# The new tokens' attention values: page values as the moving operand at four row positions

## The reference, cut to what matters

```python
def gather(pool):
    g = pool[page_table]                       # (8 samples, 2 pages, 128 rows, 8 heads, 64)
    return g.reshape((g.shape[0], g.shape[1] * g.shape[2]) + g.shape[3:])
# fox_attention, for one new token per sample
s = einsum('bqhd,bkhd->bhqk', q, k) * scale + fq - fk
p = softmax(s)
out = einsum('bhqk,bkhd->bqhd', p, v)          # (8 samples, 1, 8 heads, 64)
```

## Time and profile before

| | us |
|---|---|
| median of 3 runs (3226.53 to 3233.24) | 3230.78 |
| the profiled execution | 3236.48 |
| its span, first to last instruction | 3234.7 |
| TensorE matmul busy | 3023.7 (93%) |
| VectorE, ScalarE, GpSimd busy | 1567.6, 955.6, 1332.6 |
| mean granted TensorE clock | 0.969 |

### The profile page before, as it was taken

The page is one execution under the profiler, slowest core; times in us unless marked ns, Lnnn a source line. Parts: engine busy times, 40 slices in busy tenths (PEclk is TensorE's granted clock), DMA queues, the critical chain, the costliest instruction groups (busy, mean ns, idle before and its releaser), DMA issues.

```text
span 3234.7 us, 73556 instructions
## 1 busy us (share of the span) xinstructions
PE 3023.7 (93%) x32300; PEld 2845.5 (88%) x32300; DVE 1567.6 (48%) x2107; ACT 955.6 (30%) x1640; POOL 1332.6 (41%) x1016
## 2 busy tenths in 40 slices
PE   7999988989999999989999889999878999999997
PEld 6989856889999999978999877777777999999996
DVE  5032254237666641244322156688624866663125
ACT  4132264233111121123311246666623211111112
POOL 3322310235777743341433323333232677774320
PEclk9999998999999999999999889999989999999998
DMA  3344453322223233112422313222142122324311
GB/s 101 119 135 111 144 169 110 97 79 79 79 79 112 79 131 143 52 45 103 170 92 92 100 46 98 65 61 72 47 169 91 60 79 80 114 81 134 139 42 61
DMA packets 342471, 312.25 MB, mean 97 GB/s; under 512 B 35335, under 2 KB 303059, under 8 KB 341020
## 3 DMA queue, kind: packets, MB, share of 16 engines
q1 hardware_dynamic: 325706, 275.99, 28.3%
q10 hardware_dynamic: 16466, 31.83, 2.6%
HBM read 212.79 MB, written 94.62 MB: 95 GB/s over the span
## 4 chain that ended last, share of the span: by engine, by line
PE 43%; DVE 4%; issue 3%; ACT 1%; SPq 1%; DMA 1%; POOL 1%; ACTq 0%; DVEq 0%; POOLq 0%
PE PS L521 17%; PE PS L688 12%; PE PS L2799 2%; PE PS L2811 1%; PE PS L2805 1%; PE PS L2793 1%; DVE act_lo L2516 1%; PE PS L2919 1%; PE PS L2789 1%; PE PS L702 1%; PE PS L2785 1%; PE PS L2844 0%; SPq L496 0%; PE PS L2950 0%; PE PS L2980 0%
## 5 line engine op out<-in xcount | busy, mean ns | idle before, releaser
L521 PE MATMUL PS<-act_hi,w_hi 128*128 128x344 f32 x1992 | 641.0, 322 | 38.3 <-DVE act_lo L2150 21.2
L521 PE MATMUL PS<-act_lo,w_hi 128*128 128x344 f32 x1992 | 637.8, 320 | 0.0
L521 PE MATMUL PS<-act_hi,w_lo 128*128 128x344 f32 x1992 | 637.3, 320 | 0.0
L502 POOL CAST w_hi<-w_raw 128x1024 fp32r<-128x1024 f32 (+1 forms) x119 | 129.1, 1085 | 1078.4 <-PE PS L521 561.2
L521 PEld LDWEIGHTS PS<-act_hi,w_hi 128*128 128x128 f32 x1992 | 376.4, 189 | 43.4 <-issue 28.3
L521 PEld LDWEIGHTS PS<-act_hi,w_lo 128*128 128x128 f32 x1992 | 376.4, 189 | 0.0
L521 PEld LDWEIGHTS PS<-act_lo,w_hi 128*128 128x128 f32 x1992 | 376.4, 189 | 0.0
L688 PE MATMUL PS<-T,wq_S 128*128 128x258 f32 x2880 | 365.7, 283 | 0.0
L688 PE MATMUL PS<-act_hi,wq_A 128*128 128x258 f32 x1920 | 364.5, 282 | 0.0
L688 PEld LDWEIGHTS PS<-T,wq_S 128*128 128x128 f32 x2880 | 354.4, 189 | 0.0
L688 PEld LDWEIGHTS PS<-act_hi,wq_A 128*128 128x128 f32 x1920 | 305.4, 190 | 0.0
(11 more groups left out here) (603 smaller groups left out, 5852.0 us busy)
## 6 DMA issues: line engine op xcount, KB each, us to landing
hidd<-hid_out SPq DMA_DIRECT2D x44, 516.0 KB, 3.3
w_raw<-in_ffn_w_gate_dram SPq DMA_DIRECT2D x44, 512.0 KB, 4.8
w_raw<-in_ffn_w_up_dram SPq DMA_DIRECT2D x44, 512.0 KB, 6.0
w_raw<-in_ffn_w_down_dram SPq DMA_DIRECT2D x32, 512.0 KB, 4.1
hid_in<-hidd SPq DMA_DIRECT2D x28, 516.0 KB, 7.2
proj<-stage ACTq DMA_DIRECT2D x24, 516.0 KB, 2.7
xT<-xkeep SPq DMA_DIRECT2D x3, 4128.0 KB, 16.6
rw<-z_st SPq DMA_DIRECT2D x24, 516.0 KB, 2.8
```

Of the source, the lines that this page charges most:

```text
L502: nc.gpsimd.tensor_copy(w_hi[:, u, 0:kts, :], w_raw[:, u, 0:kts, :]).then_inc(w_hi_done, 1)
L521: mm = nc.tensor.matmul(PS[:, 3 * u + c, 0:CH], w[:, u, kt, :], x[:, kt, CH * c:CH * c + CH], start=(kt == 0 and part == 0), stop=(kt == k ...
```

## The change

In steps 28 and 31 the roles of the operands are swapped. The probabilities of one page (128 rows by 8 heads) are the stationary operand, and the page of values is the moving one, 512 columns. Four samples' results lie at the row positions 0, 32, 64 and 96 of one PSUM bank, eight rows (heads) each. Every head is multiplied with the values of all heads, so only a block diagonal of the result is wanted: VectorE multiplies with a head mask (`d_own`) into `d_mix`, and one step later (29 and 32) TensorE sums the rows of each sample and turns the result by a product with a constant (`d_seq`), 128 x 128 times 4 columns, four times. ScalarE then copies 128 x 16 into `d_of`. The marks `DV0`, `DV1` go from ScalarE to VectorE, and new marks `DG0`, `DG1` on TensorE and ScalarE take part in the ring. POOL and SP wait for `DG1` where they waited for `DV1`.

```diff
-            return names + {... 28: ["DV0"], 31: ["DV1"]}.get(j, [])
+            return names + {... 28: ["DV0"], 29: ["DG0"], 31: ["DV1"], 32: ["DG1"]}.get(j, [])
...
         def fox_end_sync(sp):
-            sp.wait_ge(FA.sem, FA["DV1"] + START)
+            sp.wait_ge(FA.sem, FA["DG1"] + START)
...
                 if j in (28, 31):
...
-                    for x in range(4):
-                        mm(PS[:, bank, 2 * (NS * x + 4 * h):2 * (NS * x + 4 * h + 4)], d_tm[:, 1024 + P * x:1024 + P * x + P],
-                           d_w2[:, x, 4 * h:4 * h + 4, :].rearrange("p b e -> p (b e)"), start=True, stop=False, skip_group_check=True)
-                        for i in range(8 * h, 8 * h + 8):
-                            b, p = i // NPAGES, i % NPAGES
-                            ins = mm(PS[:, bank, 2 * (NS * x + b):2 * (NS * x + b) + 2], d_v[i % 8][:, P * x:P * x + P],
-                                     d_pt[:, p, FH * b + 2 * x:FH * b + 2 * x + 2], start=False, stop=(i == 8 * h + 7), skip_group_check=True)
+                    mm(PS[:, bank, :], d_w2[:, h, :, :].rearrange("p b m -> p (b m)"), d_tm[:, 1024:1536], start=True, stop=False, skip_group_check=True)
+                    for p in range(NPAGES):
+                        for q in range(4):
+                            ins = mm(PS[32 * q:32 * q + FH, bank, :], d_pt[:, p, FH * (4 * h + q):FH * (4 * h + q) + FH], d_v[NPAGES * q + p][:, :],
+                                     start=False, stop=(p == NPAGES - 1), skip_group_check=True)
+                    ins.then_inc(FT.sem, 1)
+                if j in (29, 32):
+                    h = 0 if j == 29 else 1
+                    pe.wait_ge(FV.sem, FV[f"DV{h}"] + START)
+                    for x in range(4):
+                        ins = mm(PS[:, bank, 4 * x:4 * x + 4], d_mix[:, P * x:P * x + P], d_seq[:, :], start=True, stop=True)
                     ins.then_inc(FT.sem, 1)
...
-                if j in (28, 31):
-                    h = 0 if j == 28 else 1
-                    act.wait_ge(FT.sem, FT[f"DV{h}"] + START)
-                    out = PS[:, ring_bank(f"DV{h}"), 0:2 * NS * 4].rearrange("p (j b e) -> p j b e", j=4, e=2)
-                    for e in range(2):
-                        nc.scalar.copy(d_of[64 * e:64 * e + 64, :, 4 * h:4 * h + 4], out[64 * e:64 * e + 64, :, 4 * h:4 * h + 4, e]).then_inc(FA.sem, 1)
+                if j in (29, 32):
+                    h = 0 if j == 29 else 1
+                    act.wait_ge(FT.sem, FT[f"DG{h}"] + START)
+                    nc.scalar.copy(d_of[:, :, 4 * h:4 * h + 4], PS[:, ring_bank(f"DG{h}"), 0:16].rearrange("p (j b) -> p j b", j=4)).then_inc(FA.sem, 1)
...
                 if j == 27:
                     dve.wait_ge(d_wself_in, 16 + START)
-                    for x in range(4):
-                        c(tt(d_w2[:, x, :, :], ...), f"dw{x}")
+                    c(nc.vector.memset(d_w2[:, :, :, :], 0.0), "dwz")
+                    for h in range(2):
+                        c(tt(d_w2[:, h, :, 0:FH], ...), f"dw{h}")
+                    c(nc.vector.tensor_reduce(d_own[:, :], ident[:, :].rearrange("p (b t) -> p t b", b=4)[:, 0:FH, :], AX.X, ALU.add), "down")
+                    c(nc.vector.tensor_reduce(d_seq[:, :], ident[:, :].rearrange("p (b t) -> p b t", b=4)[:, :, 0:FH], AX.X, ALU.add), "dseq")
+                if j in (28, 31):
+                    h = 0 if j == 28 else 1
+                    dve.wait_ge(FT.sem, FT[f"DV{h}"] + START)
+                    if h:
+                        dve.wait_ge(FT.sem, FT["DG0"] + START)
+                    c(tt(d_mix[:, :].rearrange("p (h d) -> p h d", h=FH), PS[:, ring_bank(f"DV{h}"), :].rearrange("p (h d) -> p h d", h=FH),
+                         d_own[:, :].rearrange("p (h o) -> p h o", o=1).broadcast_to([P, FH, DH]), ALU.mult), f"DV{h}")
...
-            pool.wait_ge(FA.sem, FA["DV1"] + START)
+            pool.wait_ge(FA.sem, FA["DG1"] + START)
             split_pairs(pool, "out0", 4, KT)
```

More of the change, by code:

```diff
@@ L1266, in decoder_step @@
         d_pt = put("d_pt", [P, NPAGES, BF])
-        d_w2 = put("d_w2", [NS, 4, NS, 2])
-        assert places["d_w2"][2] <= 2 * ROW + 4 * TP
+        d_w2 = put("d_w2", [NS, 2, 4, 32])
+        d_own, d_seq = put("d_own", [P, FH]), put("d_seq", [P, 4])
+        assert places["d_seq"][2] <= 2 * ROW + 4 * TP
+        assert places["d_pr"][2] - places["d_sc"][1] >= 4 * FH * DH
+        d_mix = at("h", "d_mix", [P, FH * DH], places["d_sc"][1])
         d_page = [nc.alloc_sbuf_tensor_at(f"d_page{i}", [P, FH * DH], F32, offset=slots["w_hi" if i < 4 else "w_lo"] + 2048 * (i % 4)) for i in range(8)]
@@ L1702, in fox_tensor_names @@
                 names += [f"{n}{p + 1}.{h}" for n, h in KV_PARTS if n == "vk"[b - 1]]
-            return names + {3: ["DX0", "DX1", "DX2"], 22: ["DB"], 23: ["DS"], 26: ["DP"], 28: ["DV0"], 31: ["DV1"]}.get(j, [])
+            return names + {3: ["DX0", "DX1", "DX2"], 22: ["DB"], 23: ["DS"], 26: ["DP"], 28: ["DV0"], 29: ["DG0"], 31: ["DV1"], 32: ["DG1"]}.get(j, [])
         def fox_scalar_names(j):
@@ L1713, in fox_scalar_names @@
                 names += [f"{n}{p + 1}.{h}" for n, h in KV_PARTS if n == "vk"[b - 1]]
-            return names + {3: ["DX0", "DX1", "DX2"], 24: ["dexp"], 26: ["DP"], 28: ["dof0", "DV0"], 31: ["dof1", "DV1"]}.get(j, [])
+            return names + {3: ["DX0", "DX1", "DX2"], 24: ["dexp"], 26: ["DP"], 29: ["DG0"], 32: ["DG1"]}.get(j, [])
         FIRST_PAGE = 6
@@ L1722, in fox_vector_names @@
             names += [f"o{(j - 1) // 4}"] if j and j % 4 == 0 else []
-            names += {5: ["dqk", "dself"], 22: ["DB"], 23: ["DS", "dself8", "dmax", "dneg"], 25: ["dinv", "dpr"], 27: ["dw0", "dw1", "dw2", "dw3"]}.get(j, [])
+            names += {5: ["dqk", "dself"], 22: ["DB"], 23: ["DS", "dself8", "dmax", "dneg"], 25: ["dinv", "dpr"], 27: ["dwz", "dw0", "dw1", "down", "dseq"], 28: ["DV0"], 31: ["DV1"]}.get(j, [])
             names += [f"{n}{j - FIRST_PAGE}" for n in ("kq", "sc")] if 0 <= j - FIRST_PAGE < NP else []
@@ L1899, in sample @@
             def sample(j):
-                name = {22: "DB", 23: "DS", 26: "DP", 28: "DV0", 31: "DV1"}.get(j)
+                name = {22: "DB", 23: "DS", 26: "DP", 28: "DV0", 29: "DG0", 31: "DV1", 32: "DG1"}.get(j)
                 if name:
@@ L2087, in sample @@
                     dve.wait_ge(d_wself_in, 16 + START)
-                    for x in range(4):
-                        c(tt(d_w2[:, x, :, :], ident[0:NS, 0:NS].rearrange("p (b o) -> p b o", o=1).broadcast_to([NS, NS, 2]),
-                             d_wself[:, 2 * x:2 * x + 2].rearrange("p (o e) -> p o e", o=1).broadcast_to([NS, NS, 2]), ALU.mult), f"dw{x}")
+                    c(nc.vector.memset(d_w2[:, :, :, :], 0.0), "dwz")
+                    for h in range(2):
+                        c(tt(d_w2[:, h, :, 0:FH], ident[0:NS, 4 * h:4 * h + 4].rearrange("p (b o) -> p b o", o=1).broadcast_to([NS, 4, FH]),
+                             d_wself[:, :].rearrange("p (o e) -> p o e", o=1).broadcast_to([NS, 4, FH]), ALU.mult), f"dw{h}")
+                    c(nc.vector.tensor_reduce(d_own[:, :], ident[:, :].rearrange("p (b t) -> p t b", b=4)[:, 0:FH, :], AX.X, ALU.add), "down")
[7 more added lines that the diff above has]
+                         d_own[:, :].rearrange("p (h o) -> p h o", o=1).broadcast_to([P, FH, DH]), ALU.mult), f"DV{h}")
                 i = j - FIRST_PAGE
```

2 lines of the change are left out of this document (1 added, 1 removed).

## The result

| | before | changed | ratio |
|---|---|---|---|
| first measurement, median | 3226.72 us (5 runs) | 3210.68 us (3206.14 to 3211.64) | 0.9942 (0.9930 to 0.9955) |
| second measurement, median | 3229.36 us (17 runs) | 3213.29 us (3210.83 to 3221.31) | 0.9955 (0.9942 to 0.9969) |

What follows compares the result with a forecast made beforehand. TensorE's two pieces (26.25 us, all exposed) were taken as the bound. Terms -11.3 + 0.3 - 0.1 - 9.5 - 1.3 + 2.4 = -19.5 us against the 3230.8 us median gave 3211.3 us, range 3205 to 3221.

Steps and rivals of the forecast that it cites:

- The pieces: TensorE's value products in steps 28 and 31: 2.7 us each at full clock, 11.3 and 9.5 us less.
- The constants: VectorE's memset, products and reductions in step 27, ahead of `least(29)`: about 1.1 us, +0.3 us, bounds 0 and 0.5.
- The mask: VectorE's 128x512 product in steps 28 and 31: 0.69 us each, hidden in waits, so no cost.
- The wait ahead of DG0: Step 29: TensorE waits for ScalarE's copy, delaying `scores(31)` by 2.5 us; full-clock gains make step 30 -0.1 us.
- `product(31)`: TensorE behind the second piece: 1.73 us at full clock instead of 3.03, -1.3 us.
- The end of the stage: Up to the first `out0` tile: POOL starts later and takes turns with VectorE's `act_lo`, +2.4 us, bounds +0.4 and +4.
- The sum: All terms of the stage from the first piece to the first tile of `out0`: -19.5 us.
- the rest moves as a whole: Behind the stage: TensorE's list has no earlier date to keep, so the whole -19.5 us carries through.
- the give-back of a few us by a low clock elsewhere: A stretch elsewhere where the lower clock falls otherwise, some us in either direction; chance 0.03.

Runs made afterwards that it cites:

- the run with one: Changed kernel with all eight page products of a piece at row position 0, samples' attention values not computed: median 3221.66 us, ratio 0.9975.
- POOL's start: Changed kernel with POOL's split of the out0 weights released by TensorE's end of the second piece instead of ScalarE's copy after DG1: 3212.21 us, ratio 0.9948.
- the exchanged loops: Changed kernel with the two page-product loops exchanged, both pages of one position before the next position: median 3214.39 us, ratio 0.9945.
- the moved product: Changed kernel with DG0 (the product with `d_seq`) and its copy moved from step 29 to the end of step 30: median 3213.84 us, ratio 0.9953.
- both edits: Changed kernel with DG0 in step 30 and POOL released at the end of the second piece: median 3209.99 us, ratio 0.9945.

## Why the prediction was right

The forecast of 3211.3 us lies 0.6 us above the first median and 2.0 below the second. Its ratio to the median it was set against, 3211.3 / 3230.8 = 0.9940, lies within the first interval and just below the second. Step by step, with one profile of each kernel for the sizes:

- **The pieces.** 2.88 us where 2.7 stood. Fours at 0.43 us as written, and that the fours need four positions is shown by the run with one; the prediction's reason for them, that the diff issues the positions one after another, was wrong. The opening product takes 1.05 us in place of 0.86 plus 0.1. Both pieces together: 26.25 - 5.76 = 20.5 us less, forecast 20.8. The Trainium skill (TensorE: Matmul & The Clock Gate, Measured speedup vs the span model) gives 2.38 times for three column positions; here one position takes 0.43 us a pass and four take 0.43 us for four, 16 passes in 1.83 us in place of 6.9, 3.8 times. The measurement decides: nearly the whole factor of four. (The row positions of the output in the diff are what the prediction calls positions of the columns.)
- **The constants.** 1.19 us from the memset to `least(29)`, before 0.82 with its own work, so +0.4; +0.3 was forecast. The mask took its 0.69 us within VectorE's waits both times, as forecast. What the sum did not have: VectorE waits there for the small DMA into `d_wself`, 0.86 us before and 1.42 here. Over the profiles it is 0.81 to 1.43 us in the kernel before and its variants and 1.05 to 2.16 in the changed one and its own, so whether the change has a part in it stays open. In these two profiles the first piece begins 7.29 us after the scores of block 29 (538.75) in place of 6.38, 0.9 us more.
- **The wait ahead of DG0.** It is there: 1.64 us, released by ScalarE's copy, with `scores(31)` right behind it. They start 5.09 us after `least(30)` (550.84 to 555.93); 5.3 was forecast. The waiting scores were the right thing to name; what their delay was worth was overstated. One step later they started 2.4 us sooner and only 1.3 us came through. The sum is right even so: from the end of the first piece to the second it takes 17.80 us in place of 17.98, -0.2, and -0.1 was forecast.
- **`product(31)`.** 1.73 us, as forecast, before 3.03.
- **The end of the stage.** +1.8 us in place of +2.4. The order in the rows is the one that was played through, turn by turn: `out0` starts 7.3 us after the spread (7.4 in the prediction), and the wait for the fourth `act_lo` is there and ends 13.5 us after the spread (14.1). The eight operations in turn took 0.55 us less than was played through, nearly all of what the term is off by. POOL's start by itself is worth only 0.6 us, since an earlier start leaves turns to be taken too. The Trainium skill (SBUF — State Buffer, SBUF: two separate sides) calls the shared port pair an exclusive lock. The trace agrees, and shows besides that the two engines alternate (a cast of 2.03 us, a subtraction of 3.21).
- **The sum** of the stage from the first piece to the square of the first tile of `out0` (546.94 to 613.32, 66.4 us; now 546.04 to 592.23, 46.2 us) is -20.2 us, and -19.8 with the constants; counted from the scores of block 29, with the later DMA, it is -19.3. Forecast: -19.5.

**The step that failed** stands in the sum: "the rest moves as a whole". The medians moved by 16, and 3 to 4 us are not seen there. Part of them can be pointed at: from the scores of block 29 to the first mixing product of layer 1 it takes 920.9 us before, in both profiles, and 902.8 in the changed kernel, 18.2 us less and not 19.3. (Between the first tile and the last L716 the changed kernel wins another 0.6 us, and behind it it loses 1.7.) The stretch from the last of the FFN's opening products (L716, at 746.8 us) to the first product of the mixing of layer 1 (1441.5 us) takes 694.7 us in the five profiles in which the stage up to `out0` took 32.2 to 33.5 us: the changed kernel, the exchanged loops, POOL's start, the moved product and both edits. It takes 693.0 or 693.1 in the six in which the stage took 41 us or more: the kernel before twice, with 64 and with 128 columns, and the changed kernel with all products at one position and with two more opening products. The last two have the swapped operands, so the swapped operands alone don't cost the 1.7 us. What sets the two groups apart is when the work behind is reached: the norm below begins at 1403.0 to 1405.4 us in the five and at 1414.1 to 1427.4 in the six. That this is the cause is argued and not shown. The rows where it parts are the norm behind the FFN:

```profile
1403.45 0.88 PEld L408 LDWEIGHTS PS<-acc,ones 128*128 128x128 f32 x4 [2.75 <-DVE acc L389]
1403.46 3.01 PE L408 MATMUL PS<-acc,ones 128*128 128x344 f32 x6 [2.46 <-DVE acc L389]
...
1406.26 2.62 PE L411 MATMUL PS<-sq,ones 128*128 128x344 f32 x6
...
1408.92 1.12 ACT L371 ACTIVATE lnv<-PS,cst 128x1032 f32<-128x1032 f32 x1 [4.26 <-PE PS L411]
```

That is the changed kernel. The same work in the second profile of the kernel before:

```profile
1427.42 2.00 PE L408 MATMUL PS<-acc,ones 128*128 128x344 f32 x6 [2.47 <-DVE acc L389]
...
1429.26 1.90 PE L411 MATMUL PS<-sq,ones 128*128 128x344 f32 x6
...
1431.19 1.12 ACT L371 ACTIVATE lnv<-PS,cst 128x1032 f32<-128x1032 f32 x1 [2.58 <-PE PS L411]
```

Twelve passes stand between VectorE and ScalarE there. They took 5.47 us (1403.45 to 1408.92) at a mean clock of 0.69, and 3.77 (1427.42 to 1431.19) at the full one: 1.7 us. Over 17.3 us of this place (1404.0 to 1421.3, and 1427.9 to 1445.2 in the other) the mean granted clock is 0.61 in the changed kernel and 0.80 in the other. TensorE had just stood without work for 2.5 us in both. Another 1.4 us in the next stretch, up to the recurrence (381.4 us before, 382.8 after), I can't assign: the kernel before with 64 columns shows 382.9 there. The recurrence takes 510 to 522 us from one profile to the next whatever the kernel, which covers what is left. Why the lower clock falls where it does stays open.

The chances stood at 0.60 for the forecast, and the give-back of a few us by a low clock elsewhere was one of the named cases, at 0.03. Since the 1.7 us stand in every profile with a short stage, that case was given too little. And the forecast comes so near the first median partly by the median it was set against: 3230.8 us, 4.1 above that of the kernel before in the measurement beside the changed one.

## What to carry to other kernels

Where a product has a tiny moving operand and a wide stationary one, swap them: a piece with eight pages of 512 moving columns at four row positions took 2.88 us where one with 64 loaded passes of two columns took 12 to 14. Work out what is saved at both clock levels: more than half of the stage's gain here (12.2 of 20.6 us) was the clock that the load-bound stretch had lost. Where the lower clock fell later on differed between the kernels, by 1.7 us in one place, so compare the stretches behind it as well, and compare medians, not one profile's span.

## What the runs showed that was not expected

- The order of issue over the four positions doesn't matter: two pages at one position, then the next position (loads 0.44 us apart in fours, piece 2.91 us) equals the interleaved order (2.88 us).
- The loads of 128x128 set the pace with 128 moving columns as with two (16 loads in 1.86 us both times), and the clock stayed full in them, where with two and with 64 columns it fell in both pieces. The kernel before gains 10 us by the ratio by doing 64 times the arithmetic there.
- A cast of POOL that met VectorE's `act_lo` took 2.03 us in place of 1.04, its subtraction 3.21 and 3.26 in place of 2.35, and four `act_lo` 10.07 us in place of 6.8 in the kernel whose POOL started earlier.
- The same piece at the same place gets either clock: the first piece of the changed kernel and its variants with four positions took 2.88 to 2.91 us in four profiles and 5.53 us in two.
- The extra time behind the stage, 5.47 in place of 3.77 us for twelve passes, stood in all five profiles that reach them by 1405.4 us of the span, and in none of the six that reach them at 1414.1 or later.
